# A decoder layer with routed experts: mixer spacing, x loads, the end of tile 0 and the order of the start moved

## The reference

```python
mixed = jnp.concatenate([pool_mixer(a, ...), spatial_gating(u, v, ...)], axis=-1)
x = x + gate1 * (mixed @ w_out[l])
h = modulate(rms_norm(x, g_norm2[l]), shift2, scale2)
# per head: 16 best of each side, then 16 best of the 256 sums -> idx; gate = softmax(best)
u_e, v_e = expert_down[idx], expert_up[idx]
act = gelu(einsum('thkd,td->thk', u_e, xb))
x = x + gate2 * einsum('thk,thkd->td', gate * act, v_e)
return rms_norm(x, g_final)
```

## Time and profile before

| | |
|---|---|
| median of 3 runs | 2993.51 us (2991.59 to 3003.49) |
| the profiled execution | 2991.22 us, span 2989.4 us |
| PE, DVE, ACT, POOL busy | 1970.5 (66%), 1912.0 (64%), 1205.8 (40%), 1136.0 (38%) us |
| DMA | 1181.83 MB, mean 395 GB/s; gathers take 88.0% of 16 engines' span |
| mean granted clock of TensorE | 0.695 |
| chain that ended last | DMA 54%, PE 23%, DVE 11%, ACT 7% |

### The profile page before, as it was taken

How to read it: one execution, slowest core, us unless ns; L and a number is a source line. 1 busy time by engine, 2 the same in 40 slices (tenths; PEclk the granted TensorE clock), 3 DMA queues, 4 the chain that set the end, 5 groups by cost and what they waited for, 6 DMA issues and landing times.

```text
span 2989.4 us, 37543 instructions
## 1 busy us (share of the span) xinstructions
PE 1970.5 (66%) x12770; PEld 902.0 (30%) x12770; DVE 1912.0 (64%) x4707; ACT 1205.8 (40%) x3855; POOL 1136.0 (38%) x1032
## 2 busy tenths in 40 slices
PE   5777888767878556667656756666666666566553
PEld 4444443434534213223222312232222322222110
DVE  5775766656755465767566676667576776667544
ACT  1234444343543343434344443444334443344333
POOL 0033334234333244444444444444444444444332
PEclk9788997888888556666676566566566657565555
DMA  9599999899999999999999999999999999999997
GB/s 405 194 360 366 354 400 397 322 357 383 418 376 366 408 403 420 421 412 420 421 421 421 410 420 421 415 410 419 416 421 421 409 415 420 419 403 419 418 421 294
DMA packets 176213, 1181.83 MB, mean 395 GB/s; under 512 B 19731, under 2 KB 28947, under 8 KB 42774
## 3 DMA queue, kind: packets, MB, share of 16 engines
q0 software_dynamic: 147456, 1073.81, 88.0%
q1 hardware_dynamic: 28566, 105.63, 9.1%
HBM read 1170.98 MB, written 8.39 MB: 395 GB/s over the span
## 4 chain that ended last, share of the span: by engine, by line
DMA 54%; PE 23%; DVE 11%; ACT 7%; issue 4%; SPq 1%; POOL 0%; DVEq 0%; ACTq 0%; POOLq 0%
DMA work<-experts,expert_rows 39%; DMA weights<-experts,expert_rows 10%; PE ps_sum L748 7%; DVE work L1288 4%; PE ps_m L666 4%; PE ps_small L717 4%; DMA x_buf<-x 2%; PE ps_wide L692 2%; PE ps_m L630 2%; PE ps_m L610 2%; ACT diag L931 1%; ACT weight L926 1%; PE ps_m L621 1%; DVE weights L1288 1%; ACT act_out L924 1%
## 5 line engine op out<-in xcount | busy, mean ns | idle before, releaser
L562 POOL DMA_INDIRECT work<-experts,expert_rows x832 | 916.4, 1101 | 1520.8 <-PE ps_sum L748 1336.3
L1288 DVE CUSTOM_DVE_ANT_0 work<-work 128x1024 f32<-128x1024 f32 x832 | 1014.1, 1221 | 639.0 <-DMA work<-experts,expert_rows 635.9
L748 PE MATMUL ps_sum<-work,diag 128*32 128x256 f32 x6656 | 743.0, 531 | 714.7 <-ACT diag L931 711.2
L924 ACT ACTIVATE act_out<-act_in 128x1 f32<-128x1 f32 x1024 | 207.3, 202 | 1222.0 <-DVE act_in L1288 1205.9
L748 PEld LDWEIGHTS ps_sum<-work,diag 128*32 128x32 f32 x6656 | 153.1, 127 | 1195.5 <-ACT diag L931 1129.2
L931 ACT ACTIVATE diag<-const,weight 128x32 f32<-128x32 f32 x1024 | 329.1, 321 | 33.5
L1288 DVE CUSTOM_DVE_ANT_0 weights<-weights,work 128x1024 f32<-128x1024 f32 x192 | 234.8, 1223 | 162.1 <-DMA weights<-experts,expert_rows 158.7
L562 POOL DMA_INDIRECT weights<-experts,expert_rows x192 | 216.6, 1128 | 301.3 <-PE ps_sum L748 283.9
L748 PE MATMUL ps_sum<-weights,diag 128*32 128x256 f32 x1536 | 183.7, 566 | 211.4 <-ACT diag L931 197.0
L926 ACT ACTIVATE weight<-gate,act_out 128x1 f32<-128x1 f32 x1024 | 301.6, 295 | 33.3
L717 PE MATMUL ps_small<-h_t,weights 128*128 128x128 f32 x960 | 213.9, 392 | 0.0
(11 more groups left out here) (159 smaller groups left out, 1711.4 us busy)
## 6 DMA issues: line engine op xcount, KB each, us to landing
work<-sides SPq DMA_DIRECT2D x68, 576.0 KB, 6.4
work<-w_ada SPq DMA_DIRECT2D x12, 2048.0 KB, 23.5
work<-experts,expert_rows POOLq DMA_INDIRECT x832
weights<-sides SPq DMA_DIRECT2D x12, 576.0 KB, 31.8
weights<-w_in SPq DMA_DIRECT2D x3, 2048.0 KB, 17.5
x_buf<-x SPq DMA_DIRECT2D x8, 512.0 KB
weights<-w_out SPq DMA_DIRECT2D x2, 2048.0 KB, 35.9
x_scratch<-h_buf SPq DMA_DIRECT2D x8, 512.0 KB
```

The costliest lines, as they stand in the source:

```text
L562: nc.gpsimd.indirect_dma_start(ring[x.ring], None, experts, bass.IndirectOffsetOnAxis(ap=rows_flat[:, x.column:x.column + 1], axis=0),).th ...
L748: last = nc.tensor.matmul(ps_sum[quarter(c), x.group, :], diag[:, x.ring, :], ring[x.ring][:, D + c * QCOLS:D + (c + 1) * QCOLS], start=x. ...
L924: nc.scalar.activation(act_out[:, s:s + 1], act_in[:, s:s + 1], ACT.Gelu).then_inc(s_gelu, 1)
L1288: nc.vector.tensor_tensor_reduce(down, down, h2_spread[x.segment % 2], 1.0, 0.0, ALU.mult, ALU.add, act_in[:, x.g % TURN:x.g % TURN + 1]). ...
```

## The change

It moves work in the lists; no instruction is added or removed but one wait of SP.

- Mixers 2 to 7 start at 31, 70, 109, 150, 190, 230 instead of 29, 68, 107, 146, 184, 220.
- The ring of eight and the held loads begin at slot 268 and 269 instead of 256 and 257.
- Tile 0's end (add, squares, pair sum, root, normalization, store) comes ten slots later, by `END_LATER`; its x1 load no longer waits for the pooled matmuls (s_y). Tile 2's preparation starts at slot 36 of tile 1 instead of 24.
- Turn 1's routing starts at slot 2 instead of 5. All its four sides are done before slot 0: two ahead of tile 1's V, two after the move of turn 0's choices; ACT's exp of turn 0 comes between the pairs. Both first sides of turn 2 are loaded before the loop.

```diff
@@ -44,6 +44,7 @@
 RING_MIX = 6
 RING = 8
 MIX_TILES = 2
+LATE_SLOT = 268
 LATE_ORDER = (6, 7, 4, 5, 0, 1, 2, 3)
 
 
@@ -57,21 +58,23 @@
 WINDOWS, MEANS, GATED, POOLED, COPY_Y, PROJECT_OUT, RESIDUAL = 21, 22, 23, 24, 25, 25, 34
 MIX_STEPS = RESIDUAL + 1
 MIX_HEAD = PROJECT_A
-MIX_AT = {1: -MIX_HEAD, 2: 29, 3: 68, 4: 107, 5: 146, 6: 184, 7: 220}
+MIX_AT = {1: -MIX_HEAD, 2: 31, 3: 70, 4: 109, 5: 150, 6: 190, 7: 230}
 
 SCALE_W_SLOTS = (3, 6, 9, 12)
 
 
 STATS2, ROOT2, NORM2, TURN_H2, COPY_H2 = 0, 1, 2, 3, 4
-PREP_AT = [45] + [24] * (TILES - 1)
+PREP_AT = [45, 36] + [24] * (TILES - 2)
 SCALE_SLOT, ADD_SLOT, SQUARE_SLOT, PAIR_SUM_SLOT, ROOT_SLOT, NORM_SLOT = 0, 3, 5, 7, 9, 11
+
+END_LATER = [0, 10] + [0] * (TILES - 2)
 
 
 ROWS_STEP, SUM_STEP, GATE_STEP, SPREAD_STEP = 14, 15, 17, 18
 ROUTE_STEPS = 19
 EXP_SLOT, MOVE_SLOT = 11, 19
 SIDES_BEFORE = (20, 15, 10, 5)
-ROUTE_AT = [None, 5, 28, 50, 74, 98]
+ROUTE_AT = [None, 2, 28, 50, 74, 98]
 for _t in range(1, TILES):
     ROUTE_AT += [SLOTS * _t + s for s in (2, 28, 68, 94)][:2 if _t == TILES - 1 else 4]
 
@@ -111,7 +114,7 @@
     def __init__(self, g, batch, group, column, segment):
         self.g, self.batch, self.group, self.column, self.segment = g, batch, group, column, segment
         self.tile, self.s = g // SLOTS, g % SLOTS
-        self.ring = g % RING_MIX if g < MIX_TILES * SLOTS else LATE_ORDER[g % RING]
+        self.ring = g % RING_MIX if g < LATE_SLOT else LATE_ORDER[g % RING]
         self.fill, self.before = 0, None
         self.first = self.last = self.opens = False
 
@@ -144,8 +147,7 @@
 FIRST_SIDES = {2: 4, 3: 5}
 
 
-SIDE_AT = {(ROUTE_AT[e] - SIDES_BEFORE[b]): (e, b) for e in range(1, TURNS) for b in range(4)
-           if ROUTE_AT[e] >= SIDES_BEFORE[b]}
+SIDE_AT = {(ROUTE_AT[e] - SIDES_BEFORE[b]): (e, b) for e in range(2, TURNS) for b in range(4)}
 
 
 def streamed(e):
@@ -169,7 +171,7 @@
         uses += [(SEGMENTS[k - 1][0] + 1 + 2 * half, ("copy", k, half)) for half in range(2)]
     for t in range(1, TILES):
         uses += [(SLOTS * (t - 1) + PREP_AT[t - 1] + TURN_H2 + 2 * half, ("turn", t, half)) for half in range(2)]
-        uses += [(SLOTS * t + PAIR_SUM_SLOT, ("pair", t - 1))]
+        uses += [(SLOTS * t + PAIR_SUM_SLOT + END_LATER[t], ("pair", t - 1))]
     uses += [(SLOTS * TILES, ("pair", TILES - 1))]
     taken = {g + i for g, _ in uses for i in range(2)}
     for e in range(1, TURNS):
@@ -455,7 +457,6 @@
             def load_x1_final(t):
                 if t == 0:
                     sp.wait_ge(s_pooled, 5)
-                    sp.wait_ge(s_y, 4)
                 elif t == 1:
                     sp.wait_ge(s_pooled, TILES)
                 else:
@@ -512,7 +513,8 @@
             load_ada(GATE2, 1)
             for b in range(4):
                 load_side(1, b)
-            load_side(2, 0)
+            for b in range(2):
+                load_side(2, b)
 
             follows = {LOAD_OF[e, b]: (e, b) for e, b in LOAD_OF}
             for g in range(TILES * SLOTS):
@@ -522,7 +524,7 @@
                         store_x1(tile)
                         if tile + 1 < TILES:
                             load_x(tile + 1)
-                    if tile == 4 and g == at + POOLED + 1:
+                    if tile == 4 and g == at + MEANS + 1:
                         load_x1_final(0)
                     if tile == TILES - 1 and g == at + POOLED + 1:
                         load_x1_final(1)
@@ -532,11 +534,11 @@
                         load_side(*follows[n])
                 if t and s == ADD_SLOT + 1 and t >= MIX_TILES:
                     load_x1_final(t)
-                if t and s == NORM_SLOT + 1:
+                if t and s == NORM_SLOT + END_LATER[t] + 1:
                     store_out(t - 1)
                 if t + 1 < TILES and s == PREP_AT[t] - 8:
                     load_x1_next(t + 1)
-                if g == MIX_TILES * SLOTS + 1:
+                if g == LATE_SLOT + 1:
                     sp.wait_ge(s_o, TILES)
                     for n in range(4 * (PAIRS - 1)):
                         sp.dma_start(held[n], sides[4 + n]).then_inc(s_held, 16)
@@ -553,7 +555,7 @@
             for x in TABLE:
                 if x.opens:
                     pool.wait_ge(s_placed, x.tile * PAIRS + x.batch[-1] + 1)
-                if x.g == MIX_TILES * SLOTS:
+                if x.g == LATE_SLOT:
                     pool.wait_ge(s_o, TILES)
                 if x.before is not None:
                     pool.wait_ge(s_free, x.before + 1)
@@ -792,10 +794,13 @@
             spread_h2(0, 1)
             mixer(TURN_H, 1)
             mod_rows(GATE2)
+            for b in range(2):
+                side(1, b)
+                scores(1, b)
             for n in range(TURN_H + 1, MIX_HEAD):
                 mixer(n, 1)
             move_choices(0)
-            for b in range(3):
+            for b in range(2, 4):
                 side(1, b)
                 scores(1, b)
 
@@ -818,7 +823,7 @@
                 for what, at in WIDE_AT.items():
                     if x.g == at and what[0] == "moved":
                         move_choices(what[1])
-                if x.tile and x.s == PAIR_SUM_SLOT:
+                if x.tile and x.s == PAIR_SUM_SLOT + END_LATER[x.tile]:
                     pair_sum(x.tile - 1)
             pair_sum(TILES - 1)
 
@@ -963,8 +968,9 @@
             copy_spread(0, 1)
             for n in range(SCALE_H + 1, MIX_HEAD):
                 mixer(n, 1)
-            exp_logits(0)
-            for b in range(3):
+            for b in range(4):
+                if b == 2:
+                    exp_logits(0)
                 copy_query(1, b)
                 copy_score(1, b)
 
@@ -986,9 +992,9 @@
                     copy_score(*SIDE_AT[x.g - 4])
                 if x.g - EXP_SLOT in ROUTE_AT:
                     exp_logits(ROUTE_AT.index(x.g - EXP_SLOT))
-                if x.tile and x.s == SQUARE_SLOT:
+                if x.tile and x.s == SQUARE_SLOT + END_LATER[x.tile]:
                     square3(x.tile - 1)
-                if x.tile and x.s == ROOT_SLOT:
+                if x.tile and x.s == ROOT_SLOT + END_LATER[x.tile]:
                     root3(x.tile - 1)
             square3(TILES - 1)
             root3(TILES - 1)
@@ -1354,9 +1360,9 @@
                 dot(x)
                 if x.tile and x.s == SCALE_SLOT:
                     scale_sums(x.tile - 1)
-                if x.tile and x.s == ADD_SLOT:
+                if x.tile and x.s == ADD_SLOT + END_LATER[x.tile]:
                     add_residual2(x.tile - 1)
-                if x.tile and x.s == NORM_SLOT:
+                if x.tile and x.s == NORM_SLOT + END_LATER[x.tile]:
                     normalize(x.tile - 1)
                 if x.g in SCALE_W_SLOTS:
                     scale_w_out(SCALE_W_SLOTS.index(x.g))
```

## The result

The changed kernel takes **2950.49 us**, median of 4 runs (2949.57 to 2954.13), beside 2995.0 us (2991.59 to 3003.49) for the kernel before on the same chip: ratio 0.9849, 95% interval 0.9827 to 0.9872. That is 44.5 us. The sign and the places were right, the size was not. The profiled execution took 2951.25 us, its span is 39.9 us shorter than before's.

The account below looks back on a forecast made before the run. DMA engines were taken as the bound, full but for short holes: −26.1 us for holes, 0 start, 0 ring lead, +1 handover, about −25; 3 more for dents, −28: 2963.2 profiled, 2965.5 median, range 2950 to 2983.

Parts of the forecast that it names:

- the four waits: Slot 32's gather, tile 0's add, squares of tiles 5 and 7: removing them gains 4.1, 11.4, 6.9 and 3.7 us.
- The start's times: Before slot 0: V from 138.5 to 145.6 us, first gather 4.2 us late, slot 0's matmul near 156.
- only the rest of the wait is lost: Mixers' stage: gathers already out go on during a wait, so 37 us of waiting left 22 us of holes.
- I lean to the first, since bytes bound both: Sum: prefers the hole count, −25 us, over the slot count, −40; 3 us added for dents gives −28.
- two counts: Whole gain: −25 us from idle DMA share in the holes, or −40 from gathers at 2.90 us a slot.
- Rival A: Whole kernel: bandwidth alone decides and waits only shift bytes; 2993.5 us, less at most 8; 13 in 100.
- The start at 0: Before and around slot 0: new order of sides nets +1.2 us, taken as 0, between +7 and −5.
- turn 1's routing at −4.1: Routing from slot 2, not 5, delivers choices before slot 32's gather wants them at slot 26: −4.1 us.
- My row for slot 32: Hole at 250 us: slot 32's gather waited for turn 1's choices, 12.67 us after the one before; 4.1 us lost.
- My start ledger: Start: first gather 4.2 us late, slot 0's matmul near 156 instead of 161.66, a 3.0 us hole closed; net +1.2.
- PE is a side ahead later: After the start: PE has one side less left to do; counted within the start's 0 us.
- The handover at +1, bounded 0 to +4: Near slot 279: PE stands some 17 us for turn 11's last side; eight outstanding gathers cover it, costing +1 us.

Follow-up runs that it names:

- undo_mixers: Changed kernel with all mixers at their old slots, ring of eight from slot 256 and held loads at 257: 2962.18 us.
- tile7_lead2: Changed kernel with tile 7's mixer at slot 226 instead of 230, so its x load has two slots of lead: 2958.1 us.
- end_2_later: Changed kernel with tile 0's end 2 slots later instead of 10 and tile 2's preparation at its old slot: 2961.58 us.
- end_2_tile5_146: end_2_later with the mixers of tiles 4 and 5 back at slots 107 and 146: 2964.91 us.
- tile0_and_tile5_back: Changed kernel with tile 0's end, tile 2's preparation and the mixers of tiles 4 and 5 wholly back at their old slots: 2981.97 us.
- route5: Changed kernel with turn 1's routing at slot 5 again, the sides staying in their new order: 2952.46 us.
- held_274: Changed kernel with the twelve held loads issued at SP's slot 274 instead of 269: 2944.94 us.

## Where the prediction was right, and the step that failed

**Right.** The kernel gained where the four waits had stood, and in three of the four places because they were gone. In the changed trace the waits for x at L845 come to 3.8 us in two, and tile 0's add at 584.08 waits for nothing. No gather stage after 1100 us moved. Undoing a part brings its wait back: 6.97, 9.84, 11.30 and 13.49 us. The x load behind the stores was the cause of tile 5's wait, as read from the earlier trace rows. The start's times held: V's matmuls from 139.81 to 146.8 (138.5 to 145.6 predicted, with everything ahead some 2 us later in this execution), first gather at 148.37, slot 0's matmul at 157.70 (156). Timeline of PE in the changed kernel, against the earlier trace rows:

```profile
139.81 7.03 PE L612 MATMUL ps_m<-weights,h_t 128*128 128x512 f32 x16
146.77 0.42 PE L740 MATMUL ps_wide<-chosen_own,const 128*32 128x64 f32 x8
147.12 2.05 PE L719 MATMUL ps_small<-h_t,work 128*128 128x128 f32 x16
150.46 2.02 PE L719 MATMUL ps_small<-h_t,work 128*128 128x128 f32 x16 [0.45 <-ACT wide L916]
157.70 1.06 PE L750 MATMUL ps_sum<-work,diag 128*32 128x256 f32 x8 [4.37 <-ACT diag L936]
```

x1 of tile 2 was not late at slot 164, and the pair sum at slot 145 cost nothing that shows.

**The step that failed: "only the rest of the wait is lost", and with it "I lean to the first, since bytes bound both".** The prediction sized the waits of ACT and DVE by idle DMA share, 11.4 + 6.9 for tiles 0 and 5 and 3.7 for tile 7. The slots showed 28 and 12.3. It had two counts in all, 25 us by DMA share and 40 by slots at 2.90 us. The second has the total, 39.9 by the spans, but partly by luck: its 20 us for 550 to 650 stand against 28, its 16 for 850 to 950 against 12.3, its 4 for slot 32 against 9 that came from the sides instead, and it had nothing for the handover, which cost 5 to 6. The other half of the mechanism was read rightly: a wait on ACT or DVE stops the slots' lists. But the waits of ACT and DVE cost about all of themselves, from 0.7 to 1.3 times:

```
wait of                            us      cost, us   where read
tiles 0 and 5, kernel before    13.04+13.63   28      gain, slots 127 to 160
tile 7, kernel before           10.01         12.3    gain, slots 220 to 224
tile 7, undo_mixers              9.84         11.8    loss, slots 220 to 224
tile 7, tile7_lead2              6.97          9.2    loss, slots 226 to 228 (6.0 left at 280)
tile 0, end_2_later             11.30         12.5    loss, slots 130 to 140
tile 4, end_2_tile5_146          4.83          3.6    loss, slots 96 to 127
tile 5, tile0_and_tile5_back    13.49         10.6    loss, slots 146 to 152, against end_2_tile5_146
```

Tile 6's waits of 5.00 us (kernel before) and 4.35 (undo_mixers) can't be priced so, since the two orders of work differ most around them. The gathers already out go on, but the stage won little of that time back: its lists are as full as its transfers. I read it so from these rows; which engine's list sets the pace between the waits I did not measure, but for the stretch near slot 75 where PE was busy throughout. And busy share is not work: in the changed kernel a share of 0.97 went with 382 GB/s, and 1.02 with 422 in one stretch and 391 in another. Of 40 us, 10 were in the time of the packets, not in idle time. Rival A is refuted. The Trainium skill (Perfetto Trace Analysis, What "DMA-bound" means) says that large descriptors are what matter for a kernel bound on its DMA engines. Here these were 97% busy, packets and bytes stayed the same, and 1.5% came; so a busy share of 97% was not enough to make that the only thing that matters.

**The start at 0 and turn 1's routing at −4.1.** Their sum, 4.1 us, came out at 10.3, and nearly all of it is the order of the sides; routing earlier gave 2 by the medians and nothing at the profile, within the scatter. My row for slot 32 read POOL's wait of 12.67 us as the cause of the hole at 250. With 9.09 us of it back in route5 no slot is later, so it was not what the slots waited for there. For the kernel before that is likely, not shown: its wait was longer and met tile 2's mixer at slot 29, and the gain does grow from 8.0 to 12.6 us between slots 31 and 48. My start ledger netted the first gather's 4.2 us against the matmul's 5, and called "PE is a side ahead later" nothing; that side is the larger half of the gain up to slot 63.

**The handover at +1, bounded 0 to +4.** It costs 5.5 to 6.3 us, as held_274 gives back, and it is why the change keeps 40 us at the profile and not 45. I had put PE's wait at 17 us, and it was 29.16; the held loads' median landing went from 31.8 to 36.8 us. What I missed is who else queues behind them: DVE's x1 of tile 3, and DVE stood 25.50 us. With two engines standing no slot was finished, POOL stood 31.28 us for a free buffer, and the eight outstanding gathers ran out. By the round-robin rule that I cited (the Trainium skill, DMA: Bandwidth & Descriptors, Queues, rings and completion order) a late side slows the gathers but never stops them. While the side moves that is what the 1.02 from 1010 to 1020 shows, but once the gathers already out had landed they did stop: share 0.43.

## What to carry to other kernels

Where transfers and engines are both nearly full, price a stall of the consuming engines at about its own length (0.7 to 1.3 times here), and not in idle DMA share. Bytes not moved against the undisturbed rate came near the cost in two stretches (10.9 us for 10.6, 11.5 for 12.5) and to a third of it in a narrow one (4.3 for 11.8), so they are a check and not a price; what settles it is when the same slot ends in both traces. Before a bulk load, list everything that queues behind it on its issuing engine, for each engine that waits, and put the small urgent loads ahead: here that alone was 5.5 us. A load's lead is its measured time in the loaded queue, here mostly 11 to 13 us for 0.5 MB, and 23 behind four stores. When one part of a change is undone, look for waits that neither of the two kernels had: here one made a part look 3.6 us larger than it is.

## What the runs showed of the hardware

The time of the same 176213 packets over 16 engines was 2911.9 us before, 2901.7 in the changed kernel, and 2912.9 with tile 0 and tile 5 back, for the same work. I had taken it for a constant. It is highest in the two kernels with the most waiting, but it does not follow the waits one by one: 2902.3 in end_2_later with its 11.30 us, 2903.9 in undo_mixers with 9.84, 2905.5 in end_2_tile5_146. What makes a packet take longer these runs don't show. A bulk load in twelve issues on SP's queue held the one 0.5 MB load behind it back from its issue at 980.45 to 1020.02, 39.6 us, over three times the 11.2 us of an x load in the same trace.
